# Order of TensorE products in the feed-forward layers: each 256-column product behind its 512-column one, in place of runs of eight

## What is computed

```python
def swiglu(h, w_gate, w_up, w_down):
    a = jnp.einsum('bsd,df->bsf', h, w_gate)
    u = jnp.einsum('bsd,df->bsf', h, w_up)
    return jnp.einsum('bsf,fd->bsd', jax.nn.silu(a) * u, w_down)
```

## Time and profile before

| what | value |
|---|---|
| median of 3 runs | 2813.79 us (2813.65 to 2814.78) |
| the profiled execution | 2814.14 us, span 2812.3 us |
| TensorE matmul busy | 2792.6 us (99% of the span), 15556 matmuls |
| TensorE weight load busy | 2396.6 us (85%) |
| VectorE busy | 1921.3 us (68%) |
| ScalarE busy | 1554.0 us (55%) |
| GpSimd busy | 241.5 us (9%) |
| memory traffic | 503.82 MB, 179 GB/s on average |

### The profile page before, as it was taken

How to read it: one execution, slowest core, us unless ns; L and a number is a source line. 1 busy time by engine, 2 the same in 40 slices (tenths; PEclk the granted TensorE clock), 3 DMA queues, 4 the chain that set the end, 5 groups by cost and what they waited for, 6 DMA issues and landing times.

```text
span 2812.3 us, 40293 instructions
## 1 busy us (share of the span) xinstructions
PE 2792.6 (99%) x15556; PEld 2396.6 (85%) x15556; DVE 1921.3 (68%) x3180; ACT 1554.0 (55%) x2718; POOL 241.5 (9%) x187
## 2 busy tenths in 40 slices
PE   9999999999999999999999999999999999999998
PEld 8889888888889888888888987888888888878887
DVE  6756676747655667756568777776566687777765
ACT  6545656545545656545456556455455465655553
POOL 0010011010010011010014100110100141001100
PEclk9999999999999999999999999999999999999999
DMA  6544445555544345555554344555555554445553
GB/s 242 191 171 158 149 156 182 193 185 190 195 167 152 139 172 194 199 190 195 195 193 179 136 163 159 210 194 182 199 189 195 183 187 153 158 156 184 209 185 135
DMA packets 75055, 503.82 MB, mean 179 GB/s; under 512 B 8784, under 2 KB 10480, under 8 KB 19184
## 3 DMA queue, kind: packets, MB, share of 16 engines
q1 hardware_dynamic: 74576, 501.07, 50.2%
q10 hardware_dynamic: 288, 0.17, 0.0%
HBM read 500.12 MB, written 1.08 MB: 178 GB/s over the span
## 4 chain that ended last, share of the span: by engine, by line
PE 93%; DVE 4%; POOL 2%; issue 1%; ACT 1%; DMA 0%; SPq 0%; DVEq 0%; ACTq 0%
PE ps L1544 45%; PE ps L1579 21%; PE ps L1585 11%; PE ps L1563 9%; PE ps L1606 3%; POOL wlo L2498 2%; DVE wlo L2038 1%; PE ps L1701 1%; PE ps L1699 1%; DVE conv L2327 1%; PE ps L1726 1%; PE ps L1716 0%; PE ps L1717 0%; PE ps L1718 0%; DVE ps L2144 0%
## 5 line engine op out<-in xcount | busy, mean ns | idle before, releaser
L1777 ACT ACTIVATE whi<-raw 128x1024 fp32r<-128x1024 f32 (+3 forms) x938 | 977.5, 1045 | 600.3 <-PE ps L1544 426.1
L2038 DVE TENSOR_TENSOR wlo<-raw,whi 128x1024 fp32r<-128x1024 f32 (+2 forms) x894 | 1084.1, 1220 | 219.9 <-ACT whi L1777 218.9
L1579 PE MATMUL ps<-xT_both,whi 128*128 128x512 f32 x2560 | 641.6, 393 | 0.0
L1544 PE MATMUL ps<-whi,xT_both 128*128 128x512 f32 (+2 forms) x2336 | 628.9, 391 | 2.6 <-DVE xT_both L2061 1.6
L1579 PEld LDWEIGHTS ps<-xT_both,whi 128*128 128x128 f32 x2560 | 461.1, 189 | 82.6
L1544 PEld LDWEIGHTS ps<-whi,xT_both 128*128 128x128 f32 x2336 | 425.5, 188 | 83.7 <-issue 9.3
L1585 PEld LDWEIGHTS ps<-xT_both,wlo 128*128 128x128 f32 x2560 | 349.3, 191 | 24.9
L1585 PE MATMUL ps<-xT_both,wlo 128*128 128x256 f32 x2560 | 357.1, 282 | 0.0
L1544 PE MATMUL ps<-wlo,xT_both 128*128 128x512 f32 (+2 forms) x1168 | 354.6, 385 | 0.3 <-DVE wlo L2038 0.3
L2118 DVE TENSOR_TENSOR h<-h,ps 128x256 f32<-128x256 f32 x320 | 127.0, 418 | 203.1 <-ACT h L1826 203.1
L1544 PEld LDWEIGHTS ps<-wlo,xT_both 128*128 128x128 f32 x1168 | 218.4, 188 | 43.7 <-DVE wlo L2038 1.4
(11 more groups left out here) (315 smaller groups left out, 2526.7 us busy)
## 6 DMA issues: line engine op xcount, KB each, us to landing
raw<-in_w SPq DMA_DIRECT2D x435, 1024.0 KB, 4.8
vr<-in_vrows SPq DMA_DIRECT2D x19, 512.0 KB, 5.6
raw<-in_w SPq DMA_DIRECT2D x12, 768.0 KB, 4.3
raw<-in_w SPq DMA_DIRECT2D x10, 896.0 KB, 4.5
sums<-scratch SPq DMA_DIRECT2D x8, 512.0 KB, 4.4
raw<-in_w SPq DMA_DIRECT2D x4, 832.0 KB, 4.4
raw<-in_w SPq DMA_DIRECT2D x4, 576.0 KB, 3.7
raw<-in_w SPq DMA_DIRECT2D x4, 512.0 KB, 6.9
```

The costliest lines, as they stand in the source:

```text
L1544: made = e.matmul(bank[:, 0:c1 - c0], xs[:, kt, sl], ws[:, j * w + c0:j * w + c1], start=kt == 0 and n == 0, stop=kt == job.nk - 1 and n == 2)
L1579: e.matmul(bank[:, :].rearrange("p (n x) -> p n x", n=2), hi[:, o:o + 128], job.xt.both[:, :, kt, :], start=kt == 0, stop=False, skip_grou ...
L1777: e.activation(out, raw, ACT.Copy).then_inc(*mark("hi", i))
L2038: e.tensor_tensor(out, raw, hi.bitcast(F32), sub).then_inc(*mark("lo", i))
```

## The change

The wait for `wlo` and the narrow matmul move into the loop over k-tiles and banks. Each narrow matmul now stands directly behind the wide matmul of the same k-tile and bank. The sixteen matmuls of a piece, their operands and their outputs stay as they are; the order goes from eight wide and eight narrow to wide, narrow, wide, narrow. The wait for `wlo` is issued once, ahead of the first narrow matmul, which is now behind one wide matmul instead of eight.

```diff
@@ -1578,10 +1578,7 @@
                 o = j * w + 128 * c
                 e.matmul(bank[:, :].rearrange("p (n x) -> p n x", n=2), hi[:, o:o + 128], job.xt.both[:, :, kt, :],
                          start=kt == 0, stop=False, skip_group_check=True)
-        pe.wait_ge(*at(*lo_there))
-        for j, (_, kt, _) in enumerate(kts):
-            for c, bank in enumerate(job.outs):
-                o = j * w + 128 * c
+                pe.wait_ge(*at(*lo_there))
                 made = e.matmul(bank[:, 256:512], lo[:, o:o + 128], job.H[:, kt, :], start=False,
                                 stop=kt == job.nk - 1, skip_group_check=True)
         made.then_inc(*mark("mm", i, 1))
```

## The result

| | before | after |
|---|---|---|
| median | 2814.02 us (2813.65 to 2814.78, 6 runs) | 2825.32 us (2824.65 to 2825.6, 6 runs) |
| span of the profiled execution | 2812.3 us | 2823.7 us |
| FFN pairs, all 2560, from the starts in the trace | 894.3 us, 0.3494 a pair | 905.1 us, 0.3536 a pair |

The changed kernel takes 11.3 us more: ratio 1.004, 95% interval 1.0028 to 1.0051. I had forecast 2790.4 us, 0.8% less.

What follows compares the result with a forecast made beforehand. TensorE, busy 99% of the span, was taken as the bound. A pair at 0.2267 + 0.1133 = 0.3400 us makes a piece 2.720 instead of 2.793, so 320 x 0.073 = 23.4 us saved: 2790.4 us, range 2788 to 2818.

Steps and rivals of the forecast that it cites:

- What bounds the kernel: Whole kernel: TensorE busy 99% of the span, so only the distance between matmul starts in the FFN stream counts.
- The clean price of a pair: FFN pieces: a wide and a narrow matmul in turn take 0.2267 + 0.1133 = 0.3400 us, against 0.349 before.
- Wide matmuls ... I take the lower bound: FFN pieces: a wide matmul behind one narrow takes 0.2267 us, saving 0.027 us a piece; the upper bound was 0.236.
- Narrow matmuls at 0.113: FFN pieces: all eight narrow matmuls, each behind a wide one, take 0.113 us instead of 0.120, saving 0.047 us a piece.
- The wait at zero: FFN pieces: waiting for the lower weights 1.6 us earlier costs nothing, at most some tenths of a us once.
- the engines behind at zero: Behind each FFN piece: ScalarE and VectorE keep up and don't become the bound, so they take nothing back.
- Same bank, same columns at zero: FFN pieces: a narrow matmul adding to columns the wide one ahead has just written costs zero.
- the slower one: Rival for the FFN pairs: every change of column count costs, 0.356 us a pair, 17.6 us lost, 2831 us; chance 0.16.
- The stream never settles: Rival, one way to no change: each narrow matmul upsets the FFN stream, 0.3485 us a pair, 2812 us; no-change chance 0.24.
- The rule of the Trainium skill: Each matmul priced by its own column count, N / 2.4 + 2.5 ns: 325 ns a pair in either order.
- the side of no change: Rival for the FFN pairs: the new order leaves the time within 0.2%, 2812 or 2813.8 us; chance 0.24.

Runs made afterwards that it cites:

- The 128-column run: Changed kernel with the narrow matmul streaming 128 columns instead of 256, half of its product left out: 2790.68 us.
- e5_wait_only: Kernel before, with only the wait for the lower weights moved behind the first wide matmul, runs of eight kept: 2814.38 us beside 2814.43.
- e3_both512: Changed kernel with the matmul of lower weights also streaming 512 columns, into the whole bank: 3081.31 us.
- e15_both384: Changed kernel with both matmuls streaming 384 columns, 192 of each half, but the wide one 512 in the first k-tile: 2828.95 us.
- e1_lag: Changed kernel with each narrow matmul one pair later, so it adds to the other bank than the wide one ahead has written: 2821.66 us.
- e6_hi16: Changed kernel with only the wide matmuls, from the second k-tile on, loading 16 weight columns instead of 128 and computing 16 rows: 2808.19 us.
- e10_both16: Changed kernel with narrow matmuls, and wide ones from the second k-tile on, loading 16 weight columns instead of 128 and computing 16 rows: 2814.84 us.
- e12_n384_flat: Changed kernel with the second matmul of a pair streaming 384 columns, read in one piece from two neighbouring k-tiles: 2969.5 us.
- e6_load16: Changed kernel with only the narrow matmuls loading 16 weight columns instead of 128 and computing 16 rows: 2810.89 us.
- e8_runs4: Kernel before, with a piece's matmuls in runs of four wide and four narrow instead of eight and eight: 2816.59 us.

## Why the prediction was wrong, point by point

- **What bounds the kernel**: right. TensorE's start-to-start distances set the time, and 10.8 of the 11.4 us are in them.
- **The clean price of a pair**: the first failure. I read 0.113 for the narrow matmul behind a wide one as time saved, and 0.2267 + 0.1133 = 0.3400 as a pair's price. The first pair of a stage does take 0.340, but the saving looks like a loan: the wide matmul behind it takes 233, and 113 + 233 = 346, the clean 0.2267 + 0.120. The 128-column run shows the same with 0.060 and 0.280. In the kernel before, the loan and its return stood seven matmuls apart: 0.007 saved at the first narrow one, 0.027 paid by five wide ones. I counted them as two separate terms and removed one and multiplied the other. The loan accounts for half of the miss only, 340.0 to 346.67 ns a pair; with it alone the change would still have saved 2.7 ns a pair, 6.9 us. The other 6.67 ns, which turn the saving into a loss, are one step more in every pair, and what makes it stays open.
- **"Wide matmuls ... I take the lower bound"**: this is the step that failed in size and sign. It priced the wide matmul behind one narrow one at 0.2267, the lower bound; it measured 0.2365, just beyond the upper bound of 0.236, with single distances of 0.233, 0.236 and 0.241. The reason given, that 0.113 is half of 0.2267 and so keeps the rhythm, was tested by the change itself and fell with the second pair. It was called a choice and not a reading, and it was wrong.
- **Narrow matmuls at 0.113**: they measured 0.117 on average, in turns of 0.113, 0.117 and 0.120. That is 8 x 0.0035 = 0.03 us a piece too little. With the wide ones' 8 x 0.010 = 0.08 this makes the 0.107 us between 2.720 and 2.827.
- **The wait at zero; the engines behind at zero**: right (e5_wait_only; no idle time at the two lines).
- **Same bank, same columns at zero**: right for equal counts (e3_both512, e15_both384), not settled for unequal ones. Where banks change at every matmul (before, runs of two, four and sixteen), 1.5 to 4 steps in 8 pairs are lost (5 in one FFN), so a shared bank isn't needed for a loss. But in the two orders that lose most, the changed kernel with 8 and e1_lag with 7, nearly every matmul has a neighbour in its own bank. e6_hi16 has such neighbours too and loses nothing, with 16 output rows in the wide ones. No run alternates 512 and 256 one by one with the bank changing each time, so a share of the bank in the changed kernel's loss isn't excluded.
- **The rivals**: the slower one was right in sign, with 0.16. It priced the wide matmul at the top step, as measured, and the narrow one at 0.120, too high; so it gave 17.6 us where 11.3 were lost. The mechanism it named, that every change of count costs and that the next load has only the narrow one's time, holds by half. In this loop unequal counts are needed (e3_both512, e15_both384). A constant price for a change is ruled out by the runs of two, and a load that ends too late as the sole cause by e10_both16. "The stream never settles" had the better picture of the mechanism and too small a price, since it took its steps from transposes.
- **The rule of the Trainium skill** in "TensorE: Matmul & The Clock Gate", section "Back-to-back issue gap", as the prediction used it: its formula for the gap of an isolated matmul takes the column count alone. Used so, it stood on the side of no change, and these runs disagree: the same 512 columns take 226.7, 230, 237 or 280 ns by what stands ahead of them. The same section also says that in a real stream the spacing comes from the matmul and its weight load together. That the load has a part agrees with e6_hi16, where shorter loads alone took the pair from 353.33 to 346.67 ns.

**Shown**: the loss lies in the pairs; in this loop it needs unequal column counts (e3_both512), and none of it comes from the wait or from where the weights stand; the size of the weight loads, with the output rows, changes it, down to nothing where only the wide ones are short (e6_hi16); it is paid in whole steps of 6.667 ns, and how many depends on the pattern as a whole. **Open**: what inside of TensorE makes the step, whether neighbours in one bank add to it, whether it would stay if both counts were long enough to cover a full load (no run had that with unequal counts), why runs of two lose less than runs of four, and why one order of matmuls settles in one of two patterns. In e12_n384_flat all FFNs start alike and part behind the transposes, and both stacks have FFNs of either kind; so how the stream is taken up again decides, and not the order or the form of the weights, but how it does is open.

## What to carry to other kernels

Before two kinds of matmul are mixed, price the sequence and not the kinds: a matmul that starts early behind a longer one has borrowed from the next. Where different column counts can't be avoided, don't alternate them one by one, and put runs of one kind back to back across loop borders (here by turning every other piece, 0.1% better than before). How long the runs should be has to be measured: runs of sixteen lost least here, then two, eight and four. Equal counts of 384 or of 512 lost nothing, but they pay only where they add no columns: 512 and 512 took 267 us more. When a saving is read from one place in a pattern, look for the place in the same pattern where it is paid back, before it is multiplied.

## What was not expected of the hardware

- TensorE's steady patterns close on multiples of 6.667 ns at the full clock: 226.67, 173.33 and 120.0 ns for 512, 384 and 256 columns alone, and 340.0, 346.67, 353.33, 406.67, 413.33 and 453.33 for mixed pairs.
- One and the same loop can settle in two patterns behind a break and keeps to one until the FFN ends: 406.67 or 413.33 ns a pair in e12_n384_flat, 346.67 or 350.0 in e6_load16, 350.0 or 350.83 in e8_runs4.
- A shorter weight load can make things worse: both loads short take 349.17 ns a pair, the wide one's alone 346.67, the narrow one's alone 346.67 in six FFNs and 350.0 in two.
- A stream of equal counts can be uneven: 416 columns take 182 to 193 ns from start to start, 187.8 on average.
